# A gated encoder on one core: the input projection in seven block products instead of eight, for q, k, v and the gated units

## The chip, the core and the metric

The kernel runs on one core of one Trainium2 chip. The metric is the device time of the program in microseconds (us), from the first to the last instruction; lower is better. The engines of the core work in parallel, each through a queue of its own in a fixed order, and wait for each other at semaphores: TensorE (PE in the rows, PEld for its weight loads), VectorE (DVE), ScalarE (ACT), GpSimd (POOL) and SyncE (SP), whose queue here issues most DMA transfers.

## What is computed

One layer of an encoder on two sequences of 1024 tokens and 1024 channels (in the code: sequence 0 and 1), all in fp32:

```python
h = rmsnorm(x, g_mix) * (1 + scale1) + shift1
q, k, v, g_sw, p, gate_a, gate_b = split(h @ w_in)
ret = retention(rotary(q), rotary(k) * dk ** -0.5, v)       # both directions, 8 heads
branch_a = silu(g_sw) * (normalised(ret) * gain)
branch_b = (windowed_mean(p) - p) @ w_pool_grp * pool_scale  # 4 groups
merged = sigmoid(gate_a) * branch_a + sigmoid(gate_b) * branch_b
x = x + gate1 * (merged @ w_out)
h2 = rmsnorm(x, g_ffn) * (1 + scale2) + shift2
act, lin = split(conv3(h2 @ w_up))
x = x + gate2 * ((gelu(act) * lin) @ w_down)
y = rmsnorm(x, g_final)
```

The shifts, scales and gates come from silu(c) @ w_ada, 6 x 1024 numbers for each sequence.

## The kernel before

Each fp32 product runs as three passes on operands rounded to a shorter format: high by high, low by high, high by low, where low is the rest of the rounding. A weight piece is loaded by SP, rounded to its high by ACT, and its low is the difference that POOL makes. PE adds all passes up in PSUM, which has four slots of 128x1024 (eight banks of 128x512).

For each sequence the program has the stages mix, out, mid (the second norm), ffn and swap or last (the final norm). **mix** runs over four pairs of heads. In a pair PE does, in this order and by hand: q, k, v (192 matmuls of 512 columns, tokens as the stationary side, L1247), then the units P (the pool branch's input), GS0 (swish gate of head 0), the turns TQ and TK of q and k, KV0 (state products), SC (scores), GA0 (gate a), O0 (outputs), GB0 (gate b) with KV1 in it, O1, BB0 (pool branch of head 0), GS1 with TR0 (turning head 0's retention) in it, GA1, TR1, GB1, BB1. A unit is 48 matmuls of 512 columns (`unit`, L890). Between TR1 and BB1 there are the 48 matmuls of GB1, and the next pair's q, k, v stand behind BB1. DVE does the rotation (L2382, L2392), the states (L2431), the normalisation (L2449 statistics, L2464 centred, L2470 normed), swish and gates with a source in PSUM (L2477, L2483), branch a (L2490), branch b (L2497), the merge (L2505) and three differences of the merged blocks (L2518, four instructions). ACT makes tanh of a gate from PSUM (L1381), the weights' highs (L1371, 11 blocks of 128x1024 a pair) and the copies of v (L1637); POOL makes the lows (L1804).

The products of out, ffn-up and ffn-down already use seven block products in the place of eight: the operands are cut into 2 x 2 blocks, sums of the blocks are made for both sides, and the four result blocks are put together from seven products. In ffn a set (two column blocks, `ordinary_set`) is 7 x 12 = 84 matmuls (`product`, L921), its weight sums are POOL's (L1858 to L1868), and partial results are copied by ACT and added by DVE (L2092 and the like).

The **late modulation tiles** make shift2, scale2 and the gates: 32 loads of 128x1024 from w_ada, each times silu(c) with a sum along the row (L2237). Before, one load serves both sequences (two DVE instructions for each load), all of them in sequence 0: ten loads in pair 1, eleven in pair 2, eleven in pair 3, in a ring of four, on DVE between the merge of the pair before and the rotation. In pair 2 of sequence 0 POOL also makes the sums of w_out's blocks (out_unit).

## Time and profile before

| | us |
|---|---|
| median of three runs | 2647.01 (2646.71 to 2648.02) |
| span of the profiled execution | 2646.8 |
| PE busy | 2594.0 (98%) |
| DVE busy | 1659.9 (63%) |
| POOL busy | 1258.2 (48%) |
| ACT busy | 988.5 (37%) |

The mean granted clock of PE was 0.994 of full speed. Busy shares are averages over stages; what bounds a stage is read from the chain of the work that ended last (each piece with what released it) and from the idle time before an instruction. A matmul's duration in the rows overlaps with that of the next one; a run of matmuls gives the time of one by its count. A weight load (PEld) runs beside matmuls.

### The profile page before, as it was taken

How to read it: one execution, taken by the hardware profiler on the slowest of the kernel's cores; microseconds unless marked ns; L12 is line 12 of the kernel's file. 1: busy time of each engine (PE TensorE's matmuls, PEld its weight loads, DVE VectorE, ACT ScalarE, POOL GpSimd, SP SyncE). 2: the span in 40 equal slices, each digit the busy share in tenths (PEclk: the TensorE clock that was granted, in tenths of full speed). 3: DMA queues.
4: the chain of work that ended last, by engine and by line, in shares of the span. 5: the costliest groups of instructions: out<-in, count | busy, mean ns of one | idle time of the engine just before them, and what ended most of it. 6: DMA issues, size and time to landing. Idle time of an engine off the chain costs nothing.

```text
span 2646.8 us, 32184 instructions
## 1 busy us (share of the span) xinstructions
PE 2594.0 (98%) x12084; PEld 2131.5 (81%) x12084; DVE 1659.9 (63%) x2179; ACT 988.5 (37%) x1431; POOL 1258.2 (48%) x844
## 2 busy tenths in 40 slices
PE   7999989999999999999999999999999999999998
PEld 4888878888778888878878888888887888888886
DVE  3768686867786666665848273645768655555434
ACT  5211111114555454555621111111246545455443
POOL 1222333216377777655642122122453877775645
PEclk9999999999999999999999999999999999999998
DMA  7223153435134544497631212131251333325764
GB/s 297 91 88 125 48 197 112 150 112 154 58 128 147 167 168 158 157 337 238 184 122 49 70 33 85 33 92 43 81 147 32 104 120 104 103 93 180 213 193 146
DMA packets 300090, 341.01 MB, mean 129 GB/s; under 512 B 16288, under 2 KB 189728, under 8 KB 299936
## 3 DMA queue, kind: packets, MB, share of 16 engines
q1 hardware_dynamic: 297056, 328.46, 38.2%
q10 hardware_dynamic: 2880, 10.49, 1.0%
q8 instruction: 97, 1.59, 0.3%
q14 instruction: 57, 0.47, 0.1%
HBM read 263.39 MB, written 75.50 MB: 128 GB/s over the span
## 4 chain that ended last, share of the span: by engine, by line
PE 87%; DVE 5%; ACT 2%; DMA 2%; issue 2%; POOL 1%; SPq 1%; POOLq 0%; DVEq 0%; ACTq 0%
PE ps L921 26%; PE ps L890 23%; PE ps L1082 14%; PE ps L1247 11%; PE ps L977 5%; PE ps L1014 1%; PE ps L1275 1%; PE ps L1300 1%; PE ps L1299 1%; PE ps L1125 1%; PE ps L1312 1%; POOL y_sq L1823 1%; PE ps L1286 1%; DVE sq L2050 0%; ACT h_full L1492 0%
## 5 line engine op out<-in xcount | busy, mean ns | idle before, releaser
L1848 POOL TENSOR_TENSOR f_w<-f_ring,f_w 128x512 fp32r<-128x512 f32 x434 | 595.7, 1379 | 398.8 <-ACT f_w L1450 393.7
L921 PE MATMUL ps<-hc_hi,f_w 128*128 128x512 f32 x2240 | 690.5, 389 | 3.5 <-ACT u_act L1526 2.8
L1804 POOL TENSOR_TENSOR w_split<-w_raw,w_split 128x1024 fp32r<-128x1024 f32 x88 | 224.0, 2549 | 666.3 <-ACT w_split L1371 666.3
L890 PE MATMUL ps<-h_hi,w_split 128*128 128x512 f32 x1792 | 497.0, 394 | 6.9 <-ACT v_sb L1637 6.9
L921 PEld LDWEIGHTS ps<-hc_hi,f_w 128*128 128x128 f32 x2240 | 420.1, 188 | 92.7 <-ACT u_act L1526 3.7
L921 PE MATMUL ps<-hc_lo,f_w 128*128 128x512 f32 x1120 | 435.7, 389 | 0.0
L1082 PE MATMUL ps<-act_ring,f_w 128*128 128x512 f32 x1848 | 421.5, 390 | 3.6 <-DVE act_ring L2164 1.9
L1082 PEld LDWEIGHTS ps<-act_ring,f_w 128*128 128x128 f32 x1848 | 346.6, 188 | 77.5 <-issue 4.2
L890 PEld LDWEIGHTS ps<-h_hi,w_split 128*128 128x128 f32 x1792 | 334.2, 188 | 79.0 <-ACT v_sb L1637 7.5
L1450 ACT ACTIVATE f_w<-f_ring 128x512 fp32r<-128x512 f32 x434 | 269.9, 624 | 252.8 <-POOL f_ring L1858 109.7
L1247 PE MATMUL ps<-w_split,h_hi 128*128 128x512 f32 x1024 | 322.7, 396 | 5.5 <-DVE h_lo L2037 5.5
L890 PE MATMUL ps<-h_lo,w_split 128*128 128x512 f32 x896 | 277.0, 390 | 0.0
L2164 DVE TENSOR_TENSOR act_ring<-f_ring,act_ring 128x512 fp32r<-128x512 f32 x154 | 144.2, 942 | 178.2 <-ACT act_ring L1504 177.9
L921 PEld LDWEIGHTS ps<-hc_lo,f_w 128*128 128x128 f32 x1120 | 210.3, 188 | 43.8
L1247 PEld LDWEIGHTS ps<-w_split,h_hi 128*128 128x128 f32 x1024 | 192.7, 189 | 53.0 <-issue 10.3
L1247 PE MATMUL ps<-w_split,h_lo 128*128 128x512 f32 x512 | 200.6, 392 | 0.0
L890 PEld LDWEIGHTS ps<-h_lo,w_split 128*128 128x128 f32 x896 | 168.8, 188 | 35.7
L1381 ACT ACTIVATE bufB<-ps 128x1024 f32<-128x1024 f32 x32 | 32.8, 1024 | 369.4 <-PE ps L890 369.4
L1504 ACT ACTIVATE act_ring<-f_ring 128x512 fp32r<-128x512 f32 x154 | 97.1, 631 | 165.4 <-PE ps L1082 150.7
L977 PE MATMUL ps<-out_ring,f_w 128*128 128x512 f32 x672 | 155.2, 392 | 0.0
L1371 ACT ACTIVATE w_split<-w_raw 128x1024 fp32r<-128x1024 f32 x88 | 92.1, 1053 | 158.1 <-PE ps L1247 135.1
L977 PEld LDWEIGHTS ps<-out_ring,f_w 128*128 128x128 f32 x672 | 126.0, 188 | 27.8 <-issue 1.9
(210 smaller groups left out, 3296.7 us busy)
## 6 DMA issues: line engine op xcount, KB each, us to landing
f_ring<-in_w_up SPq DMA_DIRECT2D x160, 256.0 KB, 3.2
f_ring<-gated_out SPq DMA_DIRECT2D x154, 256.0 KB, 3.0
w_raw<-in_w_in SPq DMA_DIRECT2D x56, 512.0 KB, 3.9
gated_out<-gated_up SPq DMA_DIRECT2D x44, 512.0 KB, 4.1
f_ring<-down_sums SPq DMA_DIRECT2D x88, 256.0 KB, 3.0
gated_out<-t_gated SPq DMA_DIRECT2D x22, 768.0 KB, 6.0
f_ring<-in_w_down SPq DMA_DIRECT2D x66, 256.0 KB, 3.5
late_rows<-in_w_late SPq DMA_DIRECT2D x32, 512.0 KB, 5.6
```

The costliest lines, as they stand in the source:

```text
L890: ins = pe.matmul(ps[:, slot, b * HALF:(b + 1) * HALF], w[:, w_slot, col:col + P], a[:, k, b * HALF:(b + 1) * HALF], start=first and n == ...
L921: ins = pe.matmul(ps_row[:, half_of(bank)], a[:, cols], b, start=i in (0, 1, 3) and k == 0 and n == 0, stop=k == KQ - 1 and n == 2, skip_g ...
L977: ins = pe.matmul(ps_row[:, half_of(bank)], a[:, j * P:(j + 1) * P], b, start=i in (0, 1, 3) and c == 0 and o == 0, stop=c == PAIRS - 1 an ...
L1082: ins = pe.matmul(ps_row[:, half_of(bank)], a[:, j * P:(j + 1) * P], b, start=i in (0, 1, 3) and c == 0 and p == 0, stop=c == CHUNK_PAIRS ...
L1247: ins = pe.matmul(ps[:, slot, (t % 2) * HALF:(t % 2 + 1) * HALF], a[:, k, t * P:(t + 1) * P], w[:, ws, col:col + HALF], start=k == 0 and n ...
L1371: act.activation(w_hi[:, BLOCKS[where[0]][i][1], :], w_raw[:, i % 2, :], ACT.Copy).then_inc(hi_done.sem, 1)
L1381: act.activation(dst[:, :], ps[:, slot, :], ACT.Tanh, scale=0.5).then_inc(t.sem, 1)
L1450: act.activation(piece_slot(q)[:, 0, :], piece_raw(q), ACT.Copy).then_inc(piece_hi.sem, 1)
L1504: act.activation(act_of(where[1], m)[0], ring_slot(UP_LOADS + 2 * m + 1), ACT.Copy).then_inc(a_hi.sem, 1)
L1804: pool.tensor_tensor(w_lo[:, ws, :], w_raw[:, i % 2, :], w_hi[:, ws, :].bitcast(F32), ALU.subtract).then_inc(lo_done.sem, 1)
L1848: pool.tensor_tensor(piece_slot(q)[:, 1, :], piece_raw(q), piece_slot(q)[:, 0, :].bitcast(F32), ALU.subtract).then_inc(piece_lo.sem, 1)
L2164: dve.tensor_tensor(low, ring_slot(UP_LOADS + 2 * m + 1), high.bitcast(F32), ALU.subtract).then_inc(a_lo.sem, 1)
```

## The change

- **The gated units** (swish gate, gate a, gate b) become three sets of two 128-column blocks, each set seven products of 12 matmuls of 512 columns (`unit_product`). In the text, (s,o) is product o of set s, from (0,0) to (2,6). Four partial results of a set are copied from PSUM by ACT (`copy_unit`), three added by DVE (`unit_add(s,n)`), and tanh then reads from SBUF.
- **q, k, v** of pairs 1 to 3 become seven products of 48 matmuls of 256 columns (`qkv_products`), put together by four copies and three `qkv_add`. Pair 0 stays ordinary, as does P.
- **The side of h**: four sums of its quarters are kept on chip for the whole of mix, made in pair 0 by POOL (2), DVE (2, and 4 lows) and ACT (4 highs). h is now made in place in xT, so x is loaded again ahead of the out stage in both sequences (4 MB each; before, in sequence 0 alone).
- **Weights** come as pieces of 128x512 in a ring of five, 37 pieces and 20 sums a pair in pairs 1 to 3.
- **The late tiles** are done for each sequence apart: 16 loads in pair 1 and 16 in pair 2 of each, one DVE instruction a load, in place, in a ring of two, at six places of DVE's order (`LATE_SPOTS`). w_out's sums move to pair 3.
- **The steps behind products.** PE's small steps are put behind products by the table `behind`. bufA and bufB and the new gate_rows are dealt anew: gate a's rows of head 1 and gate b's rows of head 1 share bufA.

```diff
-LATE_RING = 4
-LATE_FROM = (0, 0, 10, 21, 32)
+LATE_RING = 2
+LATE_FROM = (0, 0, 16, 32, 32)
+LATE_SPOTS = (6, 3, 1, 2, 2, 2)
...
+            def qkv_products(where):
+                _, seq, pr = where
+                prev = pr_before(where)
+                for o in range(PRODUCTS):
+                    i = ORDER_UP[o]
...
+                    elif o == 3:
+                        pe.wait_ge(*mb_done.at(prev, 1))
+                    elif o == 6:
+                        pe.wait_ge(*q_summed.at(where, 2))
+                    else:
+                        pe.wait_ge(*q_copied.at(where, {2: 1, 4: 3, 5: 2}[o]))
+                    high, low = h_piece(seq, i)
+                    for kk in range(2):
+                        w = mix_weights(where, 2 * o + kk)
+                        for t, k2 in itertools.product(range(KQ), range(2)):
+                            rows, cols = slice(t * P, (t + 1) * P), slice(k2 * 2 * P, (k2 + 1) * 2 * P)
+                            k = 2 * kk + k2
+                            for n, (a, b) in enumerate(((high, w[0]), (high, w[1]), (low, w[0]))):
+                                ins = pe.matmul(ps[:, Q_SLOT[i], t * 2 * P:(t + 1) * 2 * P], a[:, k, rows], b[:, cols],
...
+            def unit_product(where, s, o):
...
+                elif o == 3:
+                    pe.wait_ge(*u_summed.at(where, 3 * s - 2))
+                elif o == 6:
+                    pe.wait_ge(*u_summed.at(where, 3 * s + 2))
+                else:
+                    pe.wait_ge(*u_copied.at(where, 4 * s + {2: 1, 4: 3, 5: 2}[o]))
...
                     def branch_b(h):
                         slot = slot_of(where, f"BB{h}")
-                        if h == 0:
-                            pe.wait_ge(*cent_done.at(where, 1))
-                        else:
-                            pe.wait_ge(*sw_done.at(where, 2))
+                        pe.wait_ge(*ma_done.at(where, h + 1))
...
+                    if pr:
+                        qkv_products(where)
+                        turn_qk()
+                        pool_unit(where, scores)
+                        behind = {(0, 0): (products, 0), (0, 2): (products, 1), (0, 5): (outputs, 0), (1, 3): (outputs, 1),
+                                  (1, 5): (turn_ret, 0), (2, 1): (branch_b, 0), (2, 3): (turn_ret, 1), (2, 4): (branch_b, 1)}
+                    else:
+                        first_qkv(where, pre)
+                        pool_unit(where)
+                        behind = {(0, 4): (products, 0), (0, 6): (products, 1), (1, 0): (outputs, 0), (1, 4): (outputs, 1),
+                                  (1, 6): (turn_ret, 0), (2, 1): (branch_b, 0), (2, 3): (turn_ret, 1), (2, 5): (branch_b, 1)}
+                    for s, o in itertools.product(range(MIX_SETS), range(PRODUCTS)):
+                        unit_product(where, s, o)
...
+            def copy_unit(where, s, o):
+                _, seq, pr = where
+                l, half = {0: (0, 0), 1: (1, 1), 2: (0, 1), 6: (1, 0)}[o]
+                act.wait_ge(*used.at(where, set_piece(pr, s, o) + 1))
...
+                elif (s, o) == (1, 1):
+                    act.wait_ge(*sw_done.at(where, 2))
+                elif (s, o) == (2, 1):
+                    act.wait_ge(*ga_done.at(where, 2))
```

PE at the end of pair 1 of sequence 0. Before: the last matmuls of GA1 (L890), TR1 (L1125), GB1 (first and last rows of 48 matmuls) and BB1 (L1312), then the next pair.

```order
L890 MATMUL ps<-h_hi,w_split 128x512 x2
L1125 MATMUL ps<-cst,tokb_57 128x128 [waits branch_b_done,gn_done]
L1125 MATMUL ps<-cst,tokb_57 128x128 x7
L890 MATMUL ps<-h_hi,w_split 128x512 [waits w_lo_done,w_hi_done,branch_a_done]
...
L1312 MATMUL ps<-poolU,wpool 128x512 [waits wpool_in,pool_step,swish_done]
L1312 MATMUL ps<-poolU,wpool 128x512
L1247 MATMUL ps<-w_split,h_hi 128x512 [waits tanh_a,w_lo_done,w_hi_done]
```

The same place now: products (2,2) and (2,3), TR1 (L1303), product (2,4), BB1 (L1570), products (2,5) and (2,6).

```order
L1516 MATMUL ps<-hb,f_w 128x512 [waits mix_piece_lo,mix_piece_hi,unit_copied]
...
L1516 MATMUL ps<-hb,f_w 128x512 [waits mix_piece_lo,mix_piece_hi,unit_sums]
L1516 MATMUL ps<-hb,f_w 128x512 x11
L1303 MATMUL ps<-cst,tokb_55 128x128 [waits gn_done,gn_centred]
L1303 MATMUL ps<-cst,tokb_55 128x128 x7
L1516 MATMUL ps<-ht_52,f_w 128x512 [waits mix_piece_lo,mix_piece_hi,unit_copied]
L1516 MATMUL ps<-ht_52,f_w 128x512 x11
L1570 MATMUL ps<-poolU,wpool 128x512 [waits wpool_in,pool_step,branch_a_done]
L1570 MATMUL ps<-poolU,wpool 128x512
```

TR1 had 48 matmuls ahead of and behind it; it now has 12 behind it up to BB1, and BB1 waits for branch a where it waited for the swish.

DVE at the same place. Before: centred(1), normed(1) (its rows of head 1), swish(1), gate a(1), branch a(1), branch b(1), merge(1).

```order
L2464 TENSOR_TENSOR tokb_57<-ps,mv 128x1024 [waits psum_full2]
L2470 TENSOR_TENSOR tokb_57<-tokb_57,grs 128x1024 [waits gn_centred,gn_rstd]
L2477 SCALAR_TENSOR_TENSOR bufA<-bufA,ps 128x1024 [waits tanh_swish,psum_full3]
L2483 SCALAR_TENSOR_TENSOR bufA<-bufB,bufA 128x1024 [waits swish_done,tanh_a]
L2490 SCALAR_TENSOR_TENSOR bufA<-ps,pairS,bufA 128x1024 [waits gate_a_done,psum_full0]
L2497 SCALAR_TENSOR_TENSOR bufB<-bufB,ps 128x1024 [waits tanh_b,psum_full3]
L2505 SCALAR_TENSOR_TENSOR merged_53<-bufB,pairS,bufA 128x1024 [waits branch_b_done,branch_a_done]
```

Now: two late tiles, unit_add(2,0), normed(1), gate_a(1), unit_add(2,1), branch_a(1), unit_add(2,2), branch_b(0), merge(0) and branch_b(1).

```order
L2601 SCALAR_TENSOR_TENSOR late_rows_0_74,modT<-late_rows_0_74,silu_row_72 128x1024 [waits ada_in0]
L2601 SCALAR_TENSOR_TENSOR late_rows_1_75,modT<-late_rows_1_75,silu_row_72 128x1024 [waits ada_in1]
L2814 TENSOR_TENSOR gate_rows_80<-gate_rows_80,ps 128x512 [waits unit_copied,mix_piece_used]
L2903 TENSOR_TENSOR tokb_55<-tokb_55,grs 128x1024 [waits gn_centred,gn_rstd]
L2917 SCALAR_TENSOR_TENSOR bufB<-bufA,bufB 128x1024 [waits swish_done,tanh_a]
L2814 TENSOR_TENSOR bufA<-bufA,ps 128x512 [waits unit_copied,mix_piece_used]
L2926 SCALAR_TENSOR_TENSOR bufB<-ps,pairS,bufB 128x1024 [waits gate_a_done,psum_full3]
L2814 TENSOR_TENSOR gate_rows_80<-gate_rows_80,ps 128x512 [waits unit_copied,mix_piece_used]
L2935 SCALAR_TENSOR_TENSOR gate_rows_80<-gate_rows_80,ps 128x1024 [waits tanh_b,psum_full2]
L2942 SCALAR_TENSOR_TENSOR merged_57<-gate_rows_80,pairS,swish_60 128x1024 [waits branch_b_done,branch_a_done]
L2935 SCALAR_TENSOR_TENSOR bufA<-bufA,ps 128x1024 [waits tanh_b,psum_full3]
```

The normalisation of head 1 and its gate now stand behind an addition that waits for a product of set 2 (mix_piece_used), and branch_a(1) behind a second one.

DVE at the start of a pair with late tiles, now: the last of six tiles, qkv_add(0) (L2805), half of the rotation (L2790, L2796), three tiles, qkv_add(1), one tile, qkv_add(2).

```order
L2601 SCALAR_TENSOR_TENSOR late_rows_1_75,modT<-late_rows_1_75,silu_row_72 128x1024
L2805 TENSOR_TENSOR rot<-rot,ps 128x1024
L2790 TENSOR_TENSOR bufA<-rot,cst 128x1024
...
L2797 TENSOR_TENSOR rot<-bufA,bufB 128x16x32
L2601 SCALAR_TENSOR_TENSOR late_rows_0_74,modT<-late_rows_0_74,silu_row_72 128x1024
...
L2805 TENSOR_TENSOR v_sb<-v_sb,ps 128x1024
L2601 SCALAR_TENSOR_TENSOR late_rows_1_75,modT<-late_rows_1_75,silu_row_72 128x1024
L2805 TENSOR_TENSOR rot<-rot,ps 128x1024
```

Before, twenty or twenty-two L2237 stood together ahead of the rotation (L2382), and nothing of them between the steps of q, k and v.

## Rows read from the trace of the kernel before

**Rows 1.** The page's head and first part: busy us (share of the span) xinstructions

```profile
span 2646.8 us, 32184 instructions
...
PE 2594.0 (98%) x12084; PEld 2131.5 (81%) x12084; DVE 1659.9 (63%) x2179; ACT 988.5 (37%) x1431; POOL 1258.2 (48%) x844
```

**Rows 2.** The chain that ended last, in order of time: start us, us, what

```profile
180.62 43.56 PE ps L1247 x192
...
320.34 0.02 issue
...
469.25 10.92 PE ps L1247 x48
...
771.01 345.75 PE ps L921 x1524
...
1485.71 43.56 PE ps L1247 x192
...
1552.78 1.79 PE ps L1275 x16
...
1625.41 43.56 PE ps L1247 x192
```

**Rows 3.** Windows: stretch, length, busy of PE PEld DVE ACT POOL, clock, DMA, GB/s

```profile
1485.70:1625.40 139.70, 139.70 (x698) 116.65 (x697) 74.39 (x128) 21.64 (x25) 31.15 (x13) 1.00 0.19 56
...
370.00:372.00 2.00, 1.17 (x3) 0.98 (x4) 1.95 (x5) 1.82 (x3) 0.20 (x1) 0.50 0.04 8
372.00:376.00 4.00, 4.00 (x13) 3.15 (x12) 3.85 (x4) 0.81 (x2) 3.92 (x3) 0.62 0.11 34
```

**Rows 4.** PE's timeline at 370 us; in brackets idle before and releaser

```profile
370.83 0.79 PE L890 MATMUL ps<-h_hi,w_split 128*128 128x512 f32 x1 [6.95 <-ACT v_sb L1637]
```

**Rows 5.** Weight loads of two lines: ns min/median/max, first and last start, forms

```profile
L1247 PEld LDWEIGHTS ps<-w_split,h_hi x1024: 186/188/334, 27.0 to 1807.8; 128*128 128x128 f32 x171
...
L1275 PEld LDWEIGHTS ps<-v_sb,kdp x256: 186/192/192, 106.2 to 1854.8; 128*128 128x128 f32 x128
```

**Rows 6.** Single lines of DVE, ACT and POOL, columns as in rows 5

```profile
L2470 DVE TENSOR_TENSOR tokb<-tokb,grs x16: 1224/2292/3368, 142.6 to 1876.8; 128x1024 f32<-128x1024 f32 x16
...
L2490 DVE SCALAR_TENSOR_TENSOR bufA<-ps,pairS,bufA x16: 1282/1284/1285, 149.5 to 1893.8; 128x1024 f32<-128x1024 f32 x16
...
L2092 DVE TENSOR_TENSOR u_act<-u_act,ps x40: 674/687/689, 754.3 to 2409.0; 128x512 f32<-128x512 f32 x40
...
L1637 ACT ACTIVATE v_sb<-ps x32: 575/597/599, 80.3 to 1811.5; 128x512 f32<-128x512 f32 x32
...
L1450 ACT ACTIVATE f_w<-f_ring x434: 612/622/642, 702.8 to 2613.6; 128x512 fp32r<-128x512 f32 x145
...
L1848 POOL TENSOR_TENSOR f_w<-f_ring,f_w x434: 1272/1295/2557, 704.3 to 2615.5; 128x512 fp32r<-128x512 f32 x145
```

**Rows 7.** Timeline around the start of pair 1 of sequence 1

```profile
1485.14 1.03 PE L1247 MATMUL ps<-w_split,h_hi 128*128 128x512 f32 x2
...
1485.74 1.22 DVE L2497 SCALAR_TENSOR_TENSOR bufB<-bufB,ps 128x1024 f32<-128x1024 f32 x1 [9.81 <-PE ps L1312]
1486.13 5.75 POOL L1804 TENSOR_TENSOR w_split<-w_raw,w_split 128x1024 fp32r<-128x1024 f32 x2 [20.26 <-ACT w_split L1371]
...
1489.66 2.77 DVE L2518 TENSOR_TENSOR merged_t<-merged 128x512 f32<-128x512 f32 x1
1492.35 0.68 DVE L2518 TENSOR_TENSOR merged<-merged 128x512 f32<-128x512 f32 x1
```

**Rows 8.** Late tiles: timeline in pairs 1 and 2 of sequence 0

```profile
190.80 1.22 DVE L2237 SCALAR_TENSOR_TENSOR late_prod<-late_rows,silu_rows 128x1024 f32<-128x1024 f32 x1
...
196.24 13.12 SPq L633 DMA_DIRECT2D late_rows<-in_w_late  x6
...
336.78 1.21 DVE L2237 SCALAR_TENSOR_TENSOR late_prod<-late_rows,silu_rows 128x1024 f32<-128x1024 f32 x1
```

**Rows 9.** Loads of late_rows, 512 KB each

```profile
DMA to landing us min/median/max: 3.2/5.6/8.5
```

1395 lines of the change are left out of this document (884 added, 511 removed), and 3 rows, old and new, of the table STEPS.

## The prediction

> **What bounds the kernel now.** I read the page's first part, then the chain of the work that ended last, then the busy time by stretch, and last the single rows around the places that the change touches. TensorE (PE) is busy 98% of the span, 2594.0 of 2646.8 us [rows 1]. The span is the profiled execution's own time, and it stands 0.2 us under the median of the runs, 2647.01, so I make the sum against 2647. The chain is matmuls on end: a pair of the input projection starts at 1485.71 and the next at 1625.41, 139.70 us apart [rows 2], and PE is busy for all of them, with VectorE (DVE) at 74.4, ScalarE at 21.6 and GpSimd (POOL) at 31.2 us [rows 3]. So PE work that goes is time that goes, as far as nobody else becomes late. One pair was not so: pair 2 of sequence 0 ran from 320.34 to 469.25, 148.9 us [rows 2], 9.2 more than 139.70, and PE stood for 6.95 us of it waiting for the copy of v [rows 4], because DVE did twenty-two late modulation instructions ahead of the rotation. What the change must pay for is such waits.
>
> **PE work that goes.** A 512-column matmul takes 226.9 ns in a row (43.56 us for 192, 345.75 for 1524) [rows 2]. Six ordinary gated units of 48 become three sets of 84, which is 288 against 252: 36 x 0.2269 = 8.17 us a pair, 65.3 us over eight pairs. q, k and v of pairs 1 to 3 are 192 such matmuls, 43.56 us; now they are 7 x 48 = 336 of 256 columns. The trace has no 256-column matmul. The nearest rows are 226.9 ns at 512 columns and 1.79 us for 16 of 128 columns, 112 ns [rows 2]. From 128 to 512 columns that is not a line through the ends: 512 columns at the rate of the long row is 213.3 ns at 2.4 GHz (the granted clock is 1.00 there [rows 3]) plus 13.6, so 256 columns are 106.7 + 13.6 = 120 ns (an estimate), which gives 40.4 us. The lower bound is the 112 ns that a matmul of 128 columns takes already, 37.6 us; the upper one is a load that isn't hidden, 188 ns each [rows 5], 63.2 us. I take 120, since with 512 columns the same load of 188 ns is hidden wholly and with 128 columns sixteen loads of 192 ns lie in 1.79 us. That is 3.1 us a pair, 19 us over six. P and the retention's own matmuls stay. Together **-84 us** (-101 at 112 ns, +53 at 188).
>
> By the Trainium skill's page "TensorE: Matmul & The Clock Gate", section "Back-to-back issue gap", an isolated matmul of N columns takes N/2.4 + 2.5 ns, 109 ns for 256, and the qkv stage would be 36.6 us and the gain 23 us greater. The rows are above that formula at both sizes (226.9 against 216, 112 against 56), so I don't use it.
>
> **What the other engines get.** Weights now come as 37 pieces and 20 sums a pair on POOL, 57 instructions at a median of 1.295 us [rows 6]: 74 us of a pair of 128, from 31 of 139.7. That fits. ScalarE gets 37 highs at .62 and 16 copies at .60 or twice that [rows 6]: some 40 us with its 22 of other work left out, which fits too. DVE instructions with two SBUF sources suffer, though: the merge difference L2518 that starts at 1489.66 under a POOL instruction lasts 2.77 us instead of .68 and ends with it [rows 7], and the normalising L2470 has 1.22 at least, 2.29 in the median, 3.37 at most [rows 6]. With POOL busy 58% of the pair, the mean wait is .58 x 1.29 / 2, about .4 us for each such DVE instruction (an estimate); one with a source in PSUM pays nothing (L2490 has 1.28 from the least to the most) [rows 6]. The gated units' three adds a set on DVE, .69 each [rows 6], replace nothing but lie beside PE work. All of this is hidden, except where PE's queue waits for it in order. I walked PE's queue against DVE's and ScalarE's by the order of the changed kernel; six places come out.
>
> **A. The end of each pair.** TR1 (turning head 1's retention) now stands directly behind product (2,3) and needs normed(1), which on DVE stands behind unit_add(2,0), which needs product (2,3) itself. And product (2,4) needs the copy of product (2,2), which on ScalarE stands behind the copy of (2,1) into bufA, where gate a of head 1 still lies until gate_a(1), which DVE does after normed(1). With 0 as the moment at which PE could start the next matmul: DVE starts .6 later (L1247 starts at 1485.14, L2497, which waits for the matmuls ahead of it, at 1485.74 [rows 7]), unit_add .69 to 1.3; normed(1) 1.22 + .4 to 2.9; TR1 runs .87 meanwhile; gate_a(1) 1.22 + .4 to 4.55; ScalarE: copy .60, one weight high .62, copy .60 [rows 6] to 6.45; product (2,4) starts at 6.6 and ends at 9.3. Then BB1 (pool branch, head 1), directly behind it in pairs 1 to 3, needs branch_a(1): .6 + unit_add .69 + 1.28, so it starts at 12.0. PE worked 3.6 of these 12.0 us: **8.4 us** a pair, six times; in pair 0 one more product lies ahead of BB1 and 5.7 are lost, twice. Sum **+62**. Before, the same steps had a whole unit of 11 us between them and cost nothing. Bounds: 6.5 a pair if no instruction meets POOL, 12 if normed and gate_a both take 3.37: +48 to +90.
>
> **B. TQ** waits for the second half of the rotation: product o=5 ends, .6, qkv_add 1.22, two multiplies 1.22 and two of .7, each + .4 apart from the first: 7.7 us against product o=6 of 5.8 us: 2 us x 6 = **+12** (0 to 20).
>
> **C. Late tiles.** Each sequence now does its own 32 tiles, 16 in pair 1 and 16 in pair 2, with room for two in flight, six of them ahead of the first qkv_add, three ahead of the second. DVE comes free of the pair before (branch_b, merges, sums, decay) 10.2 us after the pair's start in pair 1 of sequence 0 (190.80 after 180.62) and 16.4 in pair 2 (336.78 after 320.34) [rows 2, 8]; I take 13.5. A tile's slot is loaded again once DVE has used it: .4 to issue and landing at 3.2 to 8.5, median 5.6 [rows 9], so two tiles take 1.2 + .4 + 5 = some 7: six tiles end at 13.5 + 2 x 7 + 2.4 = 30, qkv_add and half a rotation 37, three tiles (two loaded meanwhile) 44, qkv_add(1) 45. Product o=6 would start at 6 x 5.8 = 34.6. Wait 11 in each of four pairs, **+45**. At 3.2 us it is 4, at 8.5 it is 22: +15 to +90. The rule that tells which: the landing.
>
> **D. Sets beside late tiles.** Two tiles each ahead of unit_add(0,1), (1,0) and (2,0): 19.4 us more on DVE beside its 34 us of two-source work (by 1.22 for 128x1024 and .69 for 128x512: rotation 7.7, queries 4.9, swish, gate a, normed and merge of two heads 9.8, differences 2.8, the pool's levels some 9). O1 needs qdT, which is behind them: 3 us x 4. In pair 0, product (1,4) needs the copy of (1,2) behind that of (1,1), which waits for swish(1): 5 us x 2. **+22** (0 to 45).
>
> **E. The out stage** waits for merges of pair 3 and a weight load behind them: **+7** (0 to 12). **F. Clock.** After PE's wait of 6.95 us that ended at 370.83 [rows 4] the granted clock was 0.50 and then 0.62 [rows 3]: 0.6 + 1.5 us of PE's work lost; I take 1.7 per long wait, four of them: **+7** (0 to 20). **G.** What goes: the 9.2 us of pair 2 of sequence 0: **-9**.
>
> Sum: -84 + 62 + 12 + 45 + 22 + 7 + 7 - 9 = +62, **2709 us**.
>
> **The rivals.** **1. The waits are mostly cover** (faster): A's queue holds but late tiles land in 3.2 us and nothing else waits: -84 + 48 + 15 - 9 = -30, 2617; at 112 ns a 256-column matmul, 2600. For it speaks that DMA moves 56 GB/s in such a pair [rows 3] and a load alone is quick; against it that six loads of late rows went out over 13.1 us from 196.24 [rows 8], and that A doesn't depend on loads. **2. The weight load isn't hidden** at 256 columns (slower yet): 188 ns each turns -19 into +118: 2846. It decides from the point at which the spacing is above 130 ns, where qkv gains nothing; the 16 matmuls of 128 columns at 112 ns [rows 2] speak against it. **3. The shared SBUF path** of DVE and POOL becomes the bound in pairs 1 and 2 (slower yet): 74 us of POOL + 34 + 19.4 us of two-source DVE = 127 of 128 us, so each further wait moves both; 15 to 25 us more: 2729. For it: the row at 1489.66 [rows 7]; against it, that the weights' POOL work can run some pieces ahead of PE. **4. Nothing in the end** (no change): A at 6.5, C at 8 a pair and the rest nearly hidden: 2647.
>
> Rival 3 is what the Trainium skill's page "SBUF — State Buffer", section "SBUF: two separate sides", says: a DVE instruction with two SBUF inputs and a GpSimd instruction lock each other out for a whole instruction. The row at 1489.66 agrees (2.77 us instead of .68).
>
> **How the numbers follow.** Forecast .50; rival 3 .22; rival 1 .17; rival 4 .06; rival 2 .05. The range holds the forecast with A and C between their bounds and rival 3: 2650 to 2750, and reaches down to 2635 to leave no more than 2 in 10 out. A measurement of this kernel tells 0.2%, 5 us, from no change. Faster: rival 1 and a fifth of rival 4: .18; within 0.2%: .05; slower: .77.
>
> **What would show it.** PE's rows: a wait of 3 us before the turn behind (2,3), 2.7 before (2,4), 2.7 before BB1 in every pair; none before TR1 and A falls. A wait of 4 to 22 us ahead of the last qkv product in pairs 1 and 2 alone, released by DVE whose own wait ends with a late load. 120 ns between 256-column matmuls. Pair 3 of either sequence should be the quickest, near 128.4 + 8.4 + 2 = 139 us against 139.7. If PE is busy above 97% of the new span, the forecast is wrong.

## The result and the profile after

The changed kernel takes 2764.34 us in the median of four runs (2759.66 to 2768.76) against 2646.86 of the kernel before on the same chip: a ratio of 1.0442 (95% interval 1.0427 to 1.0457), 117.5 us slower. The forecast was 2709 in a range of 2635 to 2750: the direction is right, the 62 us that it added are about half of the 117.5 that came, and the time lies above the range. The profiled execution took 2768.76 us with a span of 2766.9, 120.1 above that of before; the ledger below is made against the span.

The page's head and first part of the changed kernel, as in [rows 1]: busy us (share of the span) xinstructions.

```profile
span 2766.9 us, 34758 instructions
...
PE 2571.2 (93%) x12660; PEld 2136.7 (77%) x12660; DVE 1807.0 (65%) x2242; ACT 1146.2 (41%) x1738; POOL 1698.5 (61%) x1188
```

PE is busy only 23 us less than before, although the work taken from it is 84 us. So there are two questions: why PE stands (196 us of the span, against 53), and why it is busy so long. The windows of the six pairs with the new q, k, v answer the second. Columns as in [rows 3]: stretch, length, busy us of PE, PEld, DVE, ACT and POOL, granted clock, DMA share, GB/s.

```profile
201.90:359.64 157.74, 136.71 (x806) 119.22 (x805) 108.51 (x165) 40.93 (x63) 91.72 (x62) 0.91 0.33 103
359.64:511.36 151.72, 134.64 (x806) 117.78 (x805) 108.70 (x166) 40.95 (x63) 90.96 (x60) 0.93 0.33 107
511.36:654.68 143.32, 133.74 (x805) 116.50 (x804) 95.91 (x137) 41.99 (x65) 103.15 (x70) 0.96 0.39 132
1560.49:1718.21 157.72, 136.59 (x805) 119.12 (x804) 109.16 (x165) 40.94 (x63) 91.78 (x62) 0.91 0.32 103
1718.21:1872.60 154.39, 134.73 (x805) 117.24 (x804) 109.12 (x166) 40.83 (x63) 89.15 (x60) 0.94 0.31 98
1872.60:2015.95 143.35, 134.63 (x805) 118.09 (x804) 91.46 (x137) 42.21 (x65) 80.95 (x54) 0.95 0.25 80
```

The work of such a pair is 139.70 less 8.17 less 3.1, 128.4 us at full clock by the prediction's own count. PE is busy for 133.7 to 136.7, and the granted clock is 0.91 to 0.96 where it was 1.00 [rows 3]. The whole difference of 120, stage by stage:

| term | us | from |
|---|---|---|
| PE work taken away | -84 | as forecast |
| PE idle, pairs 1 to 3 | +90 | 908.2 long less 811.0 busy, 97.2; before 6.95 |
| PE idle, both pairs 0 | +39 | 22.3 and 22.7; before 3.9 and 2.1 |
| PE busy beyond its work at full clock | +59 | 811.0 less 6 x 128.4 is 40.4; pairs 0 11.1 and 9.4; less 2.3 before |
| out to last, both sequences | +16 | 7.3 and 8.4 |

Most of the +59 is the clock, but not all. Half of PE's busy time inside the trace's half-clock stretches is what the lower clock cost (an estimate, worked out from the trace's clock record and PE's rows): 35 us in the six pairs and 17 more than before in the pairs 0, 50 when the 2 us of before are taken off. The other 9 are PE time that the count of 128.4 lacks: experiment 10 has 129.1 to 130.8 a pair at a granted clock of 0.99 to 1.00.

Who PE waits for is in the list of its waits: engine and tile that waited <- who ended the wait: us in total, times, longest.

```profile
PE ps L1450 <- DVE v_sb L2805: 49.8, 4, 13.6
PE ps L1516 <- ACT gate_rows L1673: 18.6, 10, 2.6
PE ps L1303 <- DVE tokb L2903: 16.2, 8, 2.1
...
PE ps L1570 <- DVE bufB L2926: 11.9, 6, 2.0
PE ps L1469 <- ACT v_sb L1722: 11.0, 2, 6.4
...
PE ps L1303 <- DVE rot L2797: 6.5, 2, 3.5
PE ps L1516 <- DVE bufB L2814: 5.5, 4, 1.7
```

Line 1 is the prediction's C (four pairs with late tiles), lines 2, 3 and 4 are its A (eight of the ten times, eight and six times), L1303 behind `rot` L2797 is its B, and the last one is of its D. The other two of the ten, 2.6 us each, stand in the pairs 0 and are D's copy; they are still there in experiment 1, which undoes A. So the forecast's places are there. What it had no term for is line 5, the copy of v ahead of the pool unit, in both pairs 0.

**Place A** as it runs, PE's timeline at the end of pair 1 of sequence 0: start us, us, instruction, and in brackets the idle time before it and what ended it.

```profile
332.55 6.04 PE L1516 MATMUL ps<-hb,f_w 128*128 128x512 f32 x24
340.61 1.06 PE L1303 MATMUL ps<-cst,tokb 128*128 128x128 f32 x8 [2.01 <-DVE tokb L2903]
343.34 5.39 PE L1516 MATMUL ps<-ht,f_w 128*128 128x512 f32 x12 [1.67 <-ACT gate_rows L1673]
350.71 2.64 PE L1570 MATMUL ps<-poolU,wpool 128*128 128x512 f32 x4 [1.98 <-DVE bufB L2926]
352.36 4.72 PE L1516 MATMUL ps<-hb,f_w 128*128 128x512 f32 x12
356.92 2.88 PE L1516 MATMUL ps<-ht,f_w 128*128 128x512 f32 x12
359.64 2.56 PE L1450 MATMUL ps<-f_w,hb 128*128 128x256 f32 x20
```

Three waits of 1.7 to 2.0 us stand where 3, 2.7 and 2.7 were forecast. But twelve matmuls take 5.39 us in the third row and 2.88 in the sixth. The windows show the clock of the two stretches up to 349 (columns as above):

```profile
338.00:343.00 5.00, 1.66 (x11) 1.03 (x9) 2.96 (x3) 1.31 (x3) 0.12 (x1) 0.87 0.19 64
343.00:349.00 6.00, 5.39 (x12) 3.80 (x12) 0.23 (x1) 1.56 (x4) 4.05 (x4) 0.54 0.55 162
```

From 343 to 349 PE was granted 0.54, so nearly all of product (2,4) ran at 1.2 GHz, behind two waits of 2.01 and 1.67 us. The clock record has a half-clock stretch at this place in all eight pairs. The prediction charged a lost clock only to "long waits" like the one of 6.95 us [rows 4].

**Place C**, DVE in pair 1 of sequence 0: it starts the late tiles at 219.57, 17.7 us after the pair's start (the forecast took 13.5), and stands for loads (same columns).

```profile
219.57 1.21 DVE L2601 SCALAR_TENSOR_TENSOR late_rows<-late_rows,silu_row 128x1024 f32<-128x1024 f32 x1
...
231.38 1.23 DVE L2601 SCALAR_TENSOR_TENSOR late_rows<-late_rows,silu_row 128x1024 f32<-128x1024 f32 x1 [5.19 <-DMA late_rows<-in_w_late]
...
247.23 1.68 DVE L2601 SCALAR_TENSOR_TENSOR late_rows<-late_rows,silu_row 128x1024 f32<-128x1024 f32 x1 [3.09 <-DMA late_rows<-in_w_late]
...
248.84 1.21 DVE L2805 TENSOR_TENSOR v_sb<-v_sb,ps 128x1024 f32<-128x1024 f32 x1
```

qkv_add(1) (v) starts at 248.84 where 45 us behind the start, 246.9, had been forecast, and PE starts product o=6 at 250.10. The 48 matmuls of that product then take 8.74 us in the chain where another 48 take 5.92 (experiment 11 shows such a row): 2.8 us for the clock behind this wait.

### The profile page after: what moved, and what is told of

Its sections match the earlier page's. It is cut to its first block, busy times and chain, and to the rows that moved or that the text cites. A ratio compares the mean times of both kernels' runs of the same rounds, so it can differ in the third digit from the quotient of the medians.

```text
span 2766.9 us, 34758 instructions
## 1 busy us (share of the span) xinstructions
PE 2571.2 (93%) x12660; PEld 2136.7 (77%) x12660; DVE 1807.0 (65%) x2242; ACT 1146.2 (41%) x1738; POOL 1698.5 (61%) x1188
## 3 DMA queue, kind: packets, MB, share of 16 engines
q8 instruction: 102, 1.67, 0.3%
## 4 chain that ended last, share of the span: by engine, by line
PE 67%; DVE 18%; DMA 4%; issue 4%; ACT 4%; POOL 2%; SPq 1%; DVEq 0%; POOLq 0%; ACTq 0%
PE ps L1094 26%; PE ps L1260 13%; PE ps L1516 13%; PE ps L1155 4%; PE ps L1450 3%; PE ps L1469 3%; DMA late_rows<-in_w_late 2%; DVE state L2859 1%; DVE late_rows L2601 1%; PE ps L1192 1%; PE ps L1570 1%; PE ps L1535 1%; PE ps L1560 1%; PE ps L1359 1%; DVE merged_t L2955 1%
## 5 line engine op out<-in xcount | busy, mean ns | idle before, releaser
L2220 POOL TENSOR_TENSOR f_w<-f_ring,f_w 128x512 fp32r<-128x512 f32 x434 | 595.5, 1378 | 397.2 <-ACT f_w L1807 392.0
L2151 POOL TENSOR_TENSOR f_w<-f_ring,f_w 128x512 fp32r<-128x512 f32 x282 | 427.6, 1526 | 390.2 <-ACT f_w L1637 389.4
L1807 ACT ACTIVATE f_w<-f_ring 128x512 fp32r<-128x512 f32 x434 | 269.8, 623 | 248.9 <-POOL f_ring L2230 110.3
L1516 PE MATMUL ps<-hb,f_w 128*128 128x512 f32 x1440 | 352.3, 399 | 3.3 <-ACT v_sb L1722 1.8
L1637 ACT ACTIVATE f_w<-f_ring 128x512 fp32r<-128x512 f32 x282 | 175.1, 627 | 419.5 <-POOL f_ring L2159 156.5
L1516 PEld LDWEIGHTS ps<-hb,f_w 128*128 128x128 f32 x1440 | 272.2, 191 | 68.3 <-issue 8.2
L2533 DVE TENSOR_TENSOR act_ring<-f_ring,act_ring 128x512 fp32r<-128x512 f32 x154 | 144.8, 946 | 176.3 <-ACT act_ring L1859 176.0
L1516 PE MATMUL ps<-ht,f_w 128*128 128x512 f32 x576 | 164.9, 442 | 24.1 <-ACT gate_rows L1673 18.6
L1450 PE MATMUL ps<-f_w,hb 128*128 128x256 f32 x1440 | 174.7, 283 | 0.0
L1450 PEld LDWEIGHTS ps<-f_w,hb 128*128 128x128 f32 x1440 | 174.0, 192 | 0.5
L1155 PE MATMUL ps<-out_ring,f_w 128*128 128x512 f32 x672 | 160.7, 400 | 12.3 <-DVE out_ring L2540 10.9
L1516 PEld LDWEIGHTS ps<-ht,f_w 128*128 128x128 f32 x576 | 120.7, 214 | 55.0 <-ACT gate_rows L1673 21.3
L2246 POOL TENSOR_TENSOR f_w<-f_ring,f_w 128x512 fp32r<-128x512 f32 x56 | 82.0, 1473 | 73.6 <-ACT f_w L1824 73.4
L1450 PE MATMUL ps<-f_w,ht 128*128 128x256 f32 x576 | 80.5, 305 | 49.8 <-DVE v_sb L2805 49.8
```

The source lines that it names most:

```text
L1155: ins = pe.matmul(ps_row[:, half_of(bank)], a[:, j * P:(j + 1) * P], b, start=i in (0, 1, 3) and c == 0 and o == 0, stop=c == PAIRS - 1 an ...
L1450: ins = pe.matmul(ps[:, Q_SLOT[i], t * 2 * P:(t + 1) * 2 * P], a[:, k, rows], b[:, cols], start=i in (0, 1, 3) and k == 0 and n == 0 and t ...
L1516: ins = pe.matmul(ps_row[:, half_of(bank)], a[:, cols], b, start=i in (0, 1, 3) and k == 0 and n == 0, stop=k == KQ - 1 and n == 2, skip_g ...
L1637: act.activation(mix_out(pr, q)[:, 0, :], mix_raw(mix_load(pr, q)), ACT.Copy).then_inc(mix_hi.sem, 1)
L1807: act.activation(piece_slot(q)[:, 0, :], piece_raw(q), ACT.Copy).then_inc(piece_hi.sem, 1)
L2151: pool.tensor_tensor(out[:, 1, :], raw, out[:, 0, :].bitcast(F32), ALU.subtract).then_inc(mix_lo.sem, 1)
```

## The experiments

Each kernel is the changed one with the edit named; the code shown is an excerpt of it, in 8 to 11 against the kernel that they build on. "Pairs" are the lengths of pairs 1, 2, 3 of sequence 0 / of sequence 1; the changed kernel has 157.7, 151.7, 143.3 / 157.7, 154.4, 143.4, and its pairs 0 take 174.3 and 169.2.

**1. Place A undone.** normed(1) and gate_a(1) stand ahead of the addition that waits for product (2,3), and BB1 one product later.

```diff
                     branch_a(0)
+                    normed(1)
+                    gate_a(1)
                     late(5)
                     unit_add(2, 0)
-                    normed(1)
-                    gate_a(1)
                     unit_add(2, 1)
-... (2, 3): (turn_ret, 1), (2, 4): (branch_b, 1)}
+... (2, 3): (turn_ret, 1), (2, 5): (branch_b, 1)}
```

> One edit for the end of each pair: on DVE normed(1) and gate_a(1) stand ahead of the last two late tiles and of unit_add(2,0), where DVE waited 9 us in pair 3, and in pairs 1 to 3 BB1 stands behind product (2,5) as it does in pair 0. Theory (the three waits of PE there come from the order of DVE's queue, and the half clock behind them from the waits): the 6.9 us of waits and some 3.9 us of half clock go in each of six pairs and 6 us in each pair 0: 2764 - 77 = 2687, and pair 3 takes some 132 us instead of 143.3. Rival (DVE or the copies are late anyway, the waits form again one product later): at most a third goes, 2740. If the waits go but the granted clock stays as low (0.91 to 0.96), the clock is not theirs: 2720.

Measured: 2721.98 us, ratio 1.0284 (1.0264 to 1.0304), against 1.0442: some 42 us back, between the theory's 77 and the rival's third. Pairs 147.7, 154.2, 139.9 / 147.2, 157.0, 133.2. The same place on PE:

```profile
324.73 6.05 PE L1516 MATMUL ps<-hb,f_w 128*128 128x512 f32 x24
330.61 1.03 PE L1303 MATMUL ps<-cst,tokb 128*128 128x128 f32 x8
331.40 2.98 PE L1516 MATMUL ps<-ht,f_w 128*128 128x512 f32 x12
...
341.43 3.75 PE L1450 MATMUL ps<-f_w,hb 128*128 128x256 f32 x30
```

and its window (columns as in [rows 3]):

```profile
325.00:341.40 16.40, 16.40 (x73) 12.85 (x72) 8.98 (x10) 3.18 (x6) 7.36 (x6) 1.00 0.59 193
```

From product (2,2)'s start to the next pair it is 16.70 us (324.73 to 341.43) against 27.09 in the changed kernel (332.55 to 359.64), with the same matmuls. So place A costs 10.4 us in this pair: 5.7 of waits and 4.7 of lower clock. Taken in the same way it is 8.9 to 10.4 in the six pairs, 57 us together (50 forecast), and 6.7 and 6.8 in the pairs 0. The total of 2722 is also the 2720 of the expectation's last sentence (the waits go and the clock stays low), but that is not what happened here: the clock at this place is 1.00, and the low mean of the pairs (0.92 to 0.96 in five of them) lies around the wait for v. In pair 3 of sequence 1, which has no late tiles, all of it arrives: 143.4 to 133.2, at a clock of 0.99. But pairs 2 grow instead of shrinking, because the wait for v grew:

```profile
PE ps L1450 <- DVE v_sb L2805: 68.3, 4, 20.5
```

In pair 2 PE reaches product o=6 sooner, while DVE still has the pair before's merges, the decay and the tiles ahead. The gain is handed on to place C.

**2. The clock alone.** The waits of place A stay and are filled with matmuls on data already on chip (10, 7 and 9 of them) whose results nobody reads.

```diff
+                        if (s, o) == (2, 4):
+                            filler(7)
                         unit_product(where, s, o)
...
                             step, h = behind[s, o]
+                            if s == 2 and h == 1:
+                                filler(10 if o == 3 else 9 if o == 4 else 0)
                             step(h)
```

> The changed kernel with matmuls that fill its waits: in each pair 10 matmuls of 512 columns on h's high (into a bank that nobody reads then) ahead of TR1's wait, 7 ahead of product (2,4) and, in pairs 1 to 3, 9 ahead of BB1. They take 2.3, 1.6 and 2.0 us, less than the waits of 2.6, 1.9 and 2.4 measured from the moment at which PE was free. No wait is removed and all work stays. Theory (it is the standing still of PE that lowers the granted clock, and the half clock behind the end of a pair is worth some 4 us): the end of a pair is quicker by 3 to 4 us though PE does more, 2764 - 26 = 2738, and the granted clock there stays 1.00. Rival (the low clock has another cause, or short waits don't matter): no change, 2764, or slower by up to 5.

Measured: 2759.03, ratio 1.0423 (1.0402 to 1.0443): 5 us under the changed kernel with intervals that overlap, where 26 were expected. The half clock is gone at the place itself (columns as in [rows 3]), which takes 23.1 us (332.52 to 355.60) for 27.1 with 26 matmuls more, as expected:

```profile
339.00:345.00 6.00, 6.00 (x31) 4.73 (x30) 2.56 (x3) 2.64 (x5) 2.15 (x2) 1.00 0.07 24
```

and pair 3 of sequence 1 fell by 2.4 us to 141.0; but in pairs 1 and 2 the wait for v rose from 49.8 to 65.4 us in total. So the low clock at place A does come from PE's standing still in those short waits, and a better clock ahead of place C is paid back at C. A repair of one place can't be read in the total while the next one binds.

**3. The late tiles moved back.** Four tiles ahead of the first qkv_add in the place of six, none ahead of the second, the rest at later places.

```diff
-LATE_SPOTS = (6, 3, 1, 2, 2, 2)
+LATE_SPOTS = (4, 0, 2, 2, 2, 2, 2, 2)
```

> Only the places of the late tiles on DVE: (4, 0, 2, 2, 2, 2, 2, 2) instead of (6, 3, 1, 2, 2, 2), with two new places ahead of unit_add(2,1) and unit_add(2,2), and SP's loads in the same order. The same 32 tiles for each sequence. Theory (PE's waits of 13.5, 10.6 and the like ahead of the last qkv product come from nine tiles on DVE at two in flight): they fall to 0 to 3 us in all four pairs, and 3 us of half clock behind each go too: 2764 - 56 = 2708. Rival (the shared path of DVE and POOL is the bound in these pairs, so the waits come up in the sets instead): not under 2745.

Measured: 2774.16, ratio 1.0482 (1.0462 to 1.0503): slower than the changed kernel by 10, a miss for the theory. Pairs 152.6, 159.1, 147.3 / 151.1, 160.7, 143.2. The wait for v fell from 49.8 to 23.1 us, but PE waits at the start of pair 2 for weights (its timeline):

```profile
358.53 3.10 PE L1450 MATMUL ps<-f_w,hb 128*128 128x256 f32 x24 [1.86 <-POOL f_w L2151]
```

and SP's queue shows why: start us, us over which they went out, instructions.

```profile
324.76 21.27 SPq L771 DMA_DIRECT2D late_rows<-in_w_late  x6
346.08 4.54 SPq L800 DMA_DIRECT2D f_ring<-in_w_in  x8
```

With two slots, SP issues a late load only when DVE has used the slot. Tiles that DVE does later hold SP for 21.3 us, and the next pair's weights, which stand behind them in the same queue, go out only 7.5 us before the pair begins. The order of DVE and the order of SP must be changed together.

**4. Pair 0.** The fourth low of h's sums stands behind the queries' rotation.

```diff
-                        t_piece_low(0)
                         rope_products(0)
                         rope_products(1)
+                        t_piece_low(0)
                         t_piece_diff(0)
```

> Pair 0 alone: the first two rotations' multiplies stand ahead of the first low of h's sums on DVE, which waited 3.5 us for its high there. Theory (the pool unit of pair 0 waits 6.4 us for a copy of v that waits for these multiplies): that wait falls by 4 us and the clock comes back sooner, 5 us for each sequence, 2754. Rival (DVE's 14 us of sums lie ahead of TQ in any order and TQ waits longer by as much): 2762.

Measured: 2761.83, ratio 1.0429 (1.0408 to 1.0449). The wait ahead of P fell from 6.4 to 2.6 us and one of 4.2 came up behind it, for the same copy of v; pair 0 of sequence 0 ends at 195.9 for 201.9, that of sequence 1 takes 164.5 for 169.2. Of these 10.7 us the spans keep 6.9 (pair 3 of sequence 0 is 3.5 longer) and the medians 2.5, and the ratio of the changed kernel lies within the interval: in the total no difference is shown.

**5. Pair 0 the other way.** Each of the four lows of h's sums is made twice on DVE.

```diff
+                        dve.tensor_tensor(piece[1], source, piece[0].bitcast(F32), ALU.subtract).then_inc(low_again, 1)
+                        dve.wait_ge(low_again, 4 * seq + n + 1)
                         dve.tensor_tensor(piece[1], source, piece[0].bitcast(F32), ALU.subtract).then_inc(h_lo.sem, 1)
```

> The changed kernel with each of the four lows of h's sums in pair 0 made twice on DVE (2.2 us each, the same values). Theory (pair 0 takes 20 us more than before because DVE is the bound from the first rotation to product (0,2), and h's sums are 14 us of its queue): the three lows ahead of TQ and the fourth lengthen pair 0 by 9 to 12 us in each sequence, 2764 + 21 = 2785. Rival (pair 0's time is lost in waits between the engines, with DVE waiting as well): up to 8 us in all.

Measured: 2783.32, ratio 1.0512 (1.0496 to 1.0528), 19 us above the changed kernel; by spans 14.6, of which the two pairs 0 have 12.3 (174.3 to 178.8, 169.2 to 177.0). Four instructions of 2.28 us, 9.1 us a sequence, lengthen the pair by 4.5 and by 7.8, 12.3 together, between the theory's 18 to 24 and the rival's 8: DVE sets pair 0 for the larger part, but not alone. In the changed kernel it is busy without a gap where PE is not (from 90 to 130 us, columns as above):

```profile
90.00:130.00 40.00, 32.68 (x162) 25.91 (x162) 39.72 (x32) 15.98 (x21) 29.27 (x17) 0.93 0.26 66
```

**6. Places A, C and pair 0 together.** Edits 1 and 4; no late tiles ahead of the first two qkv_add, two at each later place, but four ahead of unit_add(2,0); and SP's order changed: the late loads in groups of two to six between the weights' loads, four of the next pair's weight loads ahead of the last two late ones.

```diff
-LATE_SPOTS = (6, 3, 1, 2, 2, 2)
+LATE_SPOTS = (0, 0, 2, 2, 2, 2, 2, 4, 2)
...
+                    for j in range(MIX_LOADS - 2, MIX_LOADS):
+                        mix_in(where, j)
+                    late = late_loads(late, 6)
+                    if pr < PAIRS - 1:
+                        for j in range(4):
+                            mix_in(("mix", seq, pr + 1), j)
+                    late = late_loads(late, 2)
```

> The order of e1_order and of e4_rope, and the late tiles dealt anew: none ahead of the first two qkv_adds, but two ahead of the third, of the sum of p, of unit_add(0,1), (1,0) and (1,1), four ahead of (2,0) and two ahead of (2,1), each pair of them loaded before; SP issues the store of the merged rows and four of the next pair's weight loads ahead of the late loads that held them up. Theory (what held the last qkv product in pairs 1 and 2 is that nine tiles wait for their loads while POOL's burst stretches DVE's merges, and DVE has 20 us to spare in set 2): pairs 1 and 2 come down to pair 3's 133 to 140 us from 147 to 157, 2722 - 60 = 2662. Rival (DVE and POOL together are the bound of these pairs): the waits come up elsewhere, not under 2700.

Measured: 2687.39, ratio 1.0145 (1.0130 to 1.0160). Pairs 144.8, 143.5, 137.0 / 144.9, 143.6, 131.7. The total came under the rival's bound of 2700, but 25 above the theory's. The wait for v no longer leads; a new one does, 26.2 us in four waits of BB1 for branch_a(1), which stands, with its addition, behind the last two tiles and their loads (DVE's timeline; two slots, refilled behind four tiles in a row):

```profile
327.82 1.23 DVE L2609 SCALAR_TENSOR_TENSOR late_rows<-late_rows,silu_row 128x1024 f32<-128x1024 f32 x1 [3.67 <-DMA late_rows<-in_w_late]
...
330.87 1.28 DVE L2934 SCALAR_TENSOR_TENSOR bufB<-ps,pairS,bufB 128x1024 f32<-128x1024 f32 x1
```

**7. Thin late tiles.** Edit 1, and each late tile loads and multiplies 128 of its 1024 columns (the shifts and gates that come from them are left incomplete).

```diff
-                sp.dma_start(late_rows[seq][n % LATE_RING][:, :],
-                             w_late[n * P:(n + 1) * P, :])
+                sp.dma_start(late_rows[seq][n % LATE_RING][:, 0:P],
+                             w_late[n * P:(n + 1) * P, 0:P])
```

> e1_order with the late tiles cut to 128 of 1024 columns, loads and DVE instructions alike (the modulation is then not the reference's): their number, places and waits stay, their cost goes. Theory (the loads and 1.2 to 2.3 us of DVE a tile make the waits of 14 and 20 us ahead of the last qkv product in e1_order): the waits fall under 3 us and pairs 1 and 2 take 133 to 138 us, 2722 - 64 = 2658. Rival (DVE is late at the start of a pair because its merges and small instructions stand under POOL's burst, tiles or not): waits of 5 us and more stay, 2685 and above.

Measured: 2667.09, ratio 1.0069 (1.0053 to 1.0086): 55 us less than edit 1 alone, so with place A gone the late tiles' size is worth 55 us. Pairs 135.9, 139.3, 136.8 / 137.0, 139.4, 133.2. That is near the theory's time, and 41.6 of the 68.3 us of waits for v are gone. Yet 26.7 stay, up to 8.4 at once, as the rival had it. DVE in pair 2, which began at 330.75:

```profile
352.45 1.38 DVE L2601 SCALAR_TENSOR_TENSOR late_rows<-late_rows,silu_row 128x128 f32<-128x128 f32 x1
...
362.46 0.29 DVE L2601 SCALAR_TENSOR_TENSOR late_rows<-late_rows,silu_row 128x128 f32<-128x128 f32 x1 [6.32 <-DMA late_rows<-in_w_late]
```

DVE comes to its first tile only 21.7 us after the pair's start, and one load of an eighth of the bytes is waited for 6.32 us; SP had issued it behind the two stores of the merged blocks. Loads of both sizes, from the DMA issues of experiments 1 (first row) and 7: KB each, median us to landing.

```profile
late_rows<-in_w_late SPq DMA_DIRECT2D x64, 512.0 KB, 3.6
late_rows<-in_w_late SPq DMA_DIRECT2D x64, 64.0 KB, 2.0
```

So the larger part of place C goes with the tiles' size. What the size doesn't explain is DVE's late arrival and the turn of a slot (slot free, issue behind the stores, landing).

**8. Spots spread.** As 6, with two tiles at each place, the last four of them behind branch_a(1), and in pair 0 the swish of head 1 ahead of its states.

```diff
-LATE_SPOTS = (0, 0, 2, 2, 2, 2, 2, 4, 2)
+LATE_SPOTS = (0, 0, 2, 2, 2, 2, 2, 2, 2, 2)
```

> e7_all with the late tiles two at a time at eight places, of which two now stand behind branch_a(1) (ahead of unit_add(2,2), and behind it), none between unit_add(2,0) and branch_a(1); in pair 0 swish(1) stands ahead of head 1's states on DVE. Theory (what is left in pairs 1 and 2 of e7_all, 6 to 7 us of waiting for branch_a(1) and 1.9 for unit_add(2,0), is where the tiles stand, and the copy of (1,2) in pair 0 waits for swish(1)): pairs 1 and 2 from 144 to some 136 us, pair 0 quicker by 3: 2687 - 38 = 2649. Rival (DVE has no room for sixteen tiles in any place): 2675 or more.

Measured: 2683.23, ratio 1.0134 (1.0119 to 1.0149). Pairs 134.2, 140.9, 148.8 / 134.2, 143.5, 140.7. Both pairs 1 are at a clock of 1.00 and 134.2 us, so DVE has room for the sixteen tiles there; the total is still as high as the rival had it. Pairs 2 and 3 wait for weights (23.8 us in nine waits), POOL being held by a load of SP that stands behind the late ones (POOL's timeline at pair 3):

```profile
468.65 1.54 POOL L2167 TENSOR_TENSOR f_ring<-f_ring 128x512 f32<-128x512 f32 x1 [6.13 <-DMA f_ring<-in_w_in]
```

**9. Fillers on top of 8**, in pair 0 (two places, nine matmuls each) and ahead of the turn of q (ten).

```diff
+                        if pr == 0 and (s, o) == (1, 4):
+                            filler(seq, 0, 9)
                         unit_product(where, s, o)
+                        if pr == 0 and (s, o) == (0, 4):
+                            filler(seq, 3, 9)
```

> e9_spots with matmuls that fill waits as in e2_fill: 10 of them ahead of TQ's wait in pairs 1 to 3, and in pair 0 nine ahead of KV0's wait and nine ahead of product (1,4), into banks that nobody reads then. Theory (each of the waits of 2 to 3 us is followed by half clock for some 3.4 us or more): ten places at 1.5 us each, 15 us under e9_spots, and a granted clock near 0.99 in pairs 1 to 3. Rival (waits are given back by DVE as in e2_fill, or the clock falls at other waits): within 4 us of e9_spots.

Measured: 2681.39, ratio 1.0129 (1.0112 to 1.0146), no difference from 8, the rival's figure. But the granted clock did not rise either: its mean is 0.982 to 0.984 in the four executions of both kernels. So this run shows neither the worth of a better clock nor that it has none; the clock fell at other waits.

**10. SP's and POOL's order mended.** As 8, with all eight of the next pair's first loads ahead of the last late loads, two places of late tiles behind an addition instead of ahead of it, and POOL's sums of w_out later (`OUT_UNIT_AT`).

```diff
-OUT_UNIT_AT = (("qkv", 0, 3), ("pool", 0, 1), ("set", 0, 5), ("set", 1, 3))
+OUT_UNIT_AT = (("qkv", 0, 3), ("set", 0, 3), ("set", 1, 0), ("set", 1, 5))
...
-                    late = late_loads(late, 6)
-                    if pr < PAIRS - 1:
-                        for j in range(4):
-                            mix_in(("mix", seq, pr + 1), j)
-                    late = late_loads(late, 2)
+                    late = late_loads(late, 4)
+                    for n in range(2):
+                        if pr < PAIRS - 1:
+                            for j in range(4 * n, 4 * n + 4):
+                                mix_in(("mix", seq, pr + 1), j)
+                        late = late_loads(late, 2)
```

> e9_spots with three moves. On SP, all eight of the next pair's weight loads stand ahead of the last two late loads (in e9_spots four stood behind them, and POOL waited 6.1 us for a load at the start of pair 3). On DVE, the late tiles of two places stand behind unit_add(0,1) and unit_add(1,1) instead of ahead. In pair 3 of sequence 0, w_out's sums of parts 2 to 4 stand later on POOL. Theory (what is left are the waits of 4.7 to 7.8 us for the low of a weight, 1.9 and 1.7 for the adds and 7.1 for a copy behind w_out's sums): pairs 2 and 3 come down to 131 to 136 us and pair 1 to 131, 2683 - 45 = 2638, under the kernel before. Rival (POOL's 74 us and DVE's queue are the bound by now, and the waits move on again): 2660 or more.

Measured over eleven runs: 2648.46 against 2645.65 of before, ratio 1.0010 (1.0001 to 1.0019). 115 of the 117.5 us are back, and nothing more: it is the best version here, and not faster than the kernel before. The time lies between the theory's 2638 and the rival's 2660. Pairs 132.1, 134.4, 137.3 / 132.1, 135.0, 135.9. Pair 1 of sequence 0 in the windows:

```profile
189.47:321.60 132.13, 129.12 (x805) 113.93 (x804) 114.83 (x161) 40.19 (x62) 90.82 (x58) 1.00 0.37 114
```

Its PE is busy for 129.1 us at full clock (129.3 in sequence 1), 0.7 above the 128.4 worked out in the prediction; no filler was needed for that clock. 7.6 us are gained over 139.70 in the pairs 1, and 2.4 to 5.4 in the pairs 2 and 3. Pair 0 eats it, in sequence 0 (first row) and in sequence 1:

```profile
27.20:189.47 162.27, 145.89 (x729) 113.76 (x729) 124.28 (x191) 65.42 (x93) 88.26 (x53) 0.97 0.33 108
1329.15:1488.19 159.04, 142.42 (x681) 115.33 (x680) 120.51 (x158) 48.06 (x71) 97.06 (x59) 0.97 0.25 74
```

They are 9.2 and 11.7 us longer than before (153.1 and 147.3), though 8.2 us of PE work is gone from each, and the stages from out on are 6.5 and 8.5 longer. Pairs 1 to 3 give back 40.7. The sum is -4.8, and the spans differ by -4.6; the profiled execution of this kernel took 2644.0, 4.5 us under the median of its runs, so in the medians nothing is left of it.

**11. One step more.** As 10, the next pair's first loads yet earlier and the first w_out sum behind the pool unit.

```diff
-OUT_UNIT_AT = (("qkv", 0, 3), ("set", 0, 3), ("set", 1, 0), ("set", 1, 5))
+OUT_UNIT_AT = (("pool", 0, 1), ("set", 0, 3), ("set", 1, 0), ("set", 1, 5))
```

> e12_units with the next pair's eight weight loads one step earlier on SP (four ahead of the late loads 10 and 11, four ahead of 12 to 15), and the first of w_out's sums on POOL behind the pool unit's pieces instead of among q, k and v's. Theory (what is left in pairs 2 and 3 are waits of 2.1 to 4.9 us for the low of a weight at the pair's start, 11 us in all): 6 to 10 us less, 2640, just under the kernel before. Rival (POOL's queue is full there whatever comes first): 2648, and a late load that waits longer could cost 3.

Measured: 2661.82, ratio 1.0057 (1.0045 to 1.0070), slower than 10, against both expectations. The waits for POOL's weights at the pair's start are gone, but pair 3 of sequence 0 has a new one and takes 146.7:

```profile
516.99 3.35 PE L1478 MATMUL ps<-hb,f_w 128*128 128x512 f32 x7 [9.74 <-ACT v_sb L1663]
```

The trace tells what holds ACT's copy of v. POOL makes the first of w_out's sums, now behind the pool unit's pieces, until 503.0; SP's store of them (L893) waits for that, six weight loads stand behind the store, POOL waits for the first of them, and ACT, whose queue is in order, stands for 19.08 us for the sum that POOL makes of it, with the copy of v next. Rows of SP, POOL and ACT:

```profile
503.03 0.37 SPq L893 DMA_DIRECT2D out_sums<-out_unit  x1
...
508.64 5.53 SPq L800 DMA_DIRECT2D f_ring<-in_w_in  x6
514.04 1.26 POOL L2168 TENSOR_TENSOR f_ring<-f_ring 128x512 f32<-128x512 f32 x1 [9.37 <-DMA f_ring<-in_w_in]
515.39 0.63 ACT L1646 ACTIVATE f_w<-f_ring 128x512 fp32r<-128x512 f32 x1 [19.08 <-POOL f_ring L2168]
```

In experiment 10 that store goes out at 487.37 and the loads from 495.30 on. By the trace, then, it is the moved sum of w_out that made the new wait; no run has that edit alone. The start of that pair, without waits, gives the spacing of 256-column matmuls: two runs of 48 start 5.76 us apart, 120 ns each.

```profile
483.97 5.92 PE L1459 MATMUL ps<-f_w,ht 128*128 128x256 f32 x48
489.73 5.92 PE L1459 MATMUL ps<-f_w,hb 128*128 128x256 f32 x48
```

With **fillers** behind product (0,4) of pair 0 on top of it:

> e14_more with nine matmuls ahead of KV0's wait of 2.6 us in pair 0, into a bank that nobody reads then. Theory (the wait is followed by half clock, and DVE is behind PE in pair 0 so that only the clock can be won): 1 to 3 us under e14_more. Rival (pair 0 is bound by DVE's queue, what PE wins it waits for later): no difference.

Measured: 2662.34, ratio 1.0054 (1.0040 to 1.0068): no difference. Here the fillers did act in their place: pair 0 of sequence 0 has a granted clock of 0.97 for 0.96, and takes 162.5 us for 162.8.

## Why the prediction was right in its direction and wrong in its size

**What bounds, and the work taken away: right.** At full clock a 256-column matmul takes 120 ns as taken (experiment 11), and pairs 1 of experiment 10 are busy for 129.1 and 129.3 us against 128.4 worked out (130.0 to 130.8 in the other pairs). Rival 2 (the load is not hidden) is ruled out: weight loads at L1450 take 192 ns in the median, beside matmuls 120 ns apart. Rivals 1 and 4 (faster, no change) are ruled out by the time of the changed kernel.

**A: right in mechanism, 34 us of idle in six pairs for 50.** 8.4 a pair had been taken, with 0.4 us for each meeting of DVE and POOL; it was 5.7 of idle in the rows, since normed(1) and gate_a(1) took 1.22 each and met nothing. The clock behind it took another 3.2 to 4.7 a pair, which is F's; with it A cost 57.

**B: 6.5 for 12**, in pairs 3 alone: where late tiles hold v back, TQ's data are ready. Experiment 3, which let v go sooner, brought it up in the others (14.7 us in six). Its terms also add up to 7.3 and not 7.7. **C: 49.8 for 45, by luck.** Two errors cancelled: the landing was 3.8 us in the median and not 5, but DVE began its tiles 15.2 to 17.7 us after the pair's start and not 13.5. **G** came as forecast.

**D: 39 us of idle in the pairs 0 where 21 had been worked out** (11 of A, 10 of D), and 5.5 in the others for 12. This step failed too: I had counted two sets beside late tiles and one copy, not the six adds, differences and lows of h that DVE got there. Of the 39, A's two waits have 7.4 and D's copy 5.2. The rest had no term; most of it are 12.8 for copies of v ahead of the pool unit and the product behind it, 5.1 for the turn of q and 5.2 for the state products. DVE is busy for 39.72 of 40 us from 90 to 130; experiment 5 showed that some two thirds of the work given to it there arrive in the pair's length, and experiment 10 that pair 0 stays 9 and 12 us above before when the other places are mended.

**F, the step that failed most: some 52 us for 7.** "I take 1.7 per long wait, four of them" took the row at 370.83 [rows 4] as the measure: only waits like that of 6.95 us cost clock (and its own rows give 0.6 + 1.5, 2.1 and not 1.7). The four long waits for v did cost 10 us by the clock record (in pair 1 8.74 for 5.92). The larger part had no term: place A, where the clock falls behind waits of 2.01 and 1.67 us (0.54 from 343 to 349), has 20 in six pairs, the waits of TQ in the pairs 3 have 4.5, and 17 lie in the two pairs 0. That experiment 2 takes the half clock away at place A itself shows the cause there; that its total didn't fall shows that the 52 are not a sum to be had alone, since a part of them lies in front of another engine's wait. In the pairs 0 the cause of the lower clock was not tested apart.

The Trainium skill, page "TensorE: Matmul & The Clock Gate", section "A second HAM failure mode: psum-queue depth-cycling", says of another kernel that frequent small idles between groups of matmuls make the clock swing between its two levels. The rows of place A agree (0.54 behind 2.01 and 1.67 us), and the forecast should have drawn on it. Not every short wait does it, though: in pair 0 of sequence 1 of the changed kernel PE waits 2.58 us ahead of the matmul at 1472.13 and 1.06 ahead of the one at 1475.16, and the clock stays at 1.00 (columns as in [rows 3]).

```profile
1468.00:1480.00 12.00, 8.35 (x44) 6.68 (x43) 11.90 (x10) 5.56 (x9) 7.86 (x5) 1.00 0.32 101
```

Pair 3 of sequence 0 in experiment 10 has a wait of 2.77 us at a clock of 1.00 too. What parts these waits from those of place A stays open.

**E: 16 for 7.** From out to swap 7.3 and from out to the end 8.4, the same within two us in the kernels here; the largest part is a wait of out's products in each sequence, 4.6 to 5.5 us, and the lower clock at it. The rest was not taken apart.

PE's busy time is 54 above F's term (45 of it clock, 9 PE time that was not counted), the idle of the pairs 0 is 18 above theirs, E 9 above and the idle of pairs 1 to 3 22 below (112 by A to D less the idle part of G, 90 measured): the prediction's 62 becomes 121, against 120. **The range** failed with F, for which it had bounds of 0 and 20.

**Rival 3** (DVE and POOL locking each other out) is seen at another place than forecast, the start of a pair. DVE's timeline in pair 2 of the changed kernel has the merge difference L2955 at 1.67 us beside a POOL instruction (L2151, 363.42 to 365.78) and at 0.68 without one:

```profile
364.66 1.67 DVE L2955 TENSOR_TENSOR merged_t<-merged 128x512 f32<-128x512 f32 x1
366.25 0.68 DVE L2955 TENSOR_TENSOR merged<-merged 128x512 f32<-128x512 f32 x1
```

and a decay mask (L2729) took 0.27 us at 374.46, but 1.31 in the same place of experiment 7. DVE came to its tiles 15.2 to 17.7 us after the pair's start in the changed kernel and 21.7 and 25.7 in pair 2 of experiments 7 and 1. Laid against the shortest duration of the same instruction in the same trace, DVE's instructions ahead of the first tile are 6.1 to 8.6 us longer in the four pairs of the changed kernel (an estimate of what the meetings cost); in the kernel before it was 3.4 and 9.7 in the two pairs at the same place, so most of this was there already. No run took POOL's share away, so its part of place C stays open. (The prediction's row at 1489.66 doesn't end with POOL's: it ends 0.55 us behind it, 1492.43 against 1491.88 [rows 7], about the 0.68 that such an instruction takes alone.)

## What to carry to other kernels

When work is taken from the engine that binds, walk the queues that feed it with the new spacing: a step of DVE that may run early should stand ahead of the one that waits for the last product, and the order of loads in the one DMA queue must follow each move of their users. Two waits of 2 us close together on TensorE, in every pair, cost here nearly as much again in the clock behind them (3.2 to 4.7 us for 5.7): give such places a term and bounds of their own, for there are other waits of that size that cost none. A repaired place whose gain is taken by the next wait says nothing about its worth in the total; mend the chain of places, then measure.

Two things stay open. No run has the gated units' seven products without those of q, k and v, or the other way round, so what each part alone would give isn't known. And pair 0, with its sums of h, keeps what pairs 1 to 3 gain.

## What the runs showed of the hardware

- The granted clock fell to 0.54 for 6 us behind two waits of 2.01 and 1.67 us, and twelve matmuls of 512 columns took 5.39 us for 2.88. With dummy matmuls in the same gaps it stayed at 1.00. Behind waits of 2.58 and 1.06 us in another pair, and one of 2.77 in experiment 10, it stayed at 1.00 as well.
- 256-column fp32 matmuls in a row: 120 ns each, with their weight load of 192 ns hidden.
- A load of 64 KB landed in 2.0 us in the median and one of 512 KB in 3.6. The single 64 KB load that was waited for longest, 6.32 us, had been issued behind two stores of the same queue.
- A load that waits for its slot holds all loads behind it in SP's queue: six late loads went out over 21.27 us, and the eight weight loads behind them waited (experiment 3).
